# Norm boundaries of a one-core kernel: the last two weight pieces tile by tile, tile-step engine orders, rows turned by a diagonal

## The reference

```python
for i in range(2):
    h = _rmsnorm(x, norm_gains[i, 0])
    h = rwkv7_time_mix(h) if i == 0 else sgu_mixer(h)
    x = x + _rmsnorm(h, norm_gains[i, 1])
    h = _rmsnorm(x, norm_gains[i, 2])
    h = (silu(h @ w_gate) * (h @ w_up)) @ w_down
    x = x + _rmsnorm(h, norm_gains[i, 3])
h = rms_norm(x, norm1_g) * (1 + sc1) + sh1
x = x + g1 * (attention(h) @ w_out)
h2 = rms_norm(x, norm2_g) * (1 + sc2) + sh2
x = x + g2 * peer_ffn(h2)            # 128 experts for each token
```

## Time and profile before

| | us |
|---|---|
| median of 3 runs | 3378.89 (3374.46 to 3381.36) |
| the profiled execution's own time | 3387.03 |
| its span | 3385.0 |
| PE busy in it | 3175.8 (94%) |
| DVE, ACT, POOL busy | 2050.3, 1287.1, 776.2 |
| DMA, mean | 159 GB/s |

### The profile page before, as it was taken

How to read it: one execution, slowest core, us unless ns; L and a number is a source line. 1 busy time by engine, 2 the same in 40 slices (tenths; PEclk the granted TensorE clock), 3 DMA queues, 4 the chain that set the end, 5 groups by cost and what they waited for, 6 DMA issues and landing times.

```text
span 3385.0 us, 42343 instructions
## 1 busy us (share of the span) xinstructions
PE 3175.8 (94%) x16625; PEld 2715.6 (80%) x16625; DVE 2050.3 (61%) x3698; ACT 1287.1 (38%) x2171; POOL 776.2 (23%) x495
## 2 busy tenths in 40 slices
PE   8878999988999898999989999999999997999999
PEld 6456988977888776888878577999999896887777
DVE  5485656554332444333247655888888685887777
ACT  4454434434232323322234433335445452333332
POOL 0000011000000020000000300377676752354453
PEclk9888999999999987999999599999999998999999
DMA  3022112133333321333322002378878888999997
GB/s 132 24 77 75 57 57 69 57 106 93 95 99 97 97 80 57 94 99 96 97 81 83 3 26 94 101 255 290 304 267 304 281 295 304 360 340 350 329 354 272
DMA packets 229208, 537.63 MB, mean 159 GB/s; under 512 B 22337, under 2 KB 88129, under 8 KB 227474
## 3 DMA queue, kind: packets, MB, share of 16 engines
q1 hardware_dynamic: 191570, 398.57, 35.6%
q0 software_dynamic: 37440, 136.36, 11.0%
HBM read 482.40 MB, written 52.46 MB: 158 GB/s over the span
## 4 chain that ended last, share of the span: by engine, by line
PE 66%; DVE 13%; DMA 11%; ACT 4%; POOL 3%; issue 2%; SPq 1%; DVEq 0%; ACTq 0%
PE bank L339 22%; PE bank L342 14%; PE bank L2174 8%; DMA gl<-acts 6%; DMA eu<-in_peer_u 4%; PE bank L2602 3%; POOL etl L2162 3%; DVE vsl L2646 2%; PE bank L952 2%; DVE y_row L2219 2%; PE bank L962 2%; PE bank L1749 2%; PE bank L2331 1%; PE bank L916 1%; PE bank L904 1%
## 5 line engine op out<-in xcount | busy, mean ns | idle before, releaser
L294 DVE TENSOR_TENSOR wl<-raw,wh 128x1024 fp32r<-128x1024 f32 (+3 forms) x239 | 294.0, 1233 | 674.0 <-ACT wh L279 673.8
L279 ACT CAST wh<-raw 128x1024 fp32r<-128x1024 f32 (+3 forms) x239 | 247.1, 1036 | 676.5 <-PE bank L339 363.8
L2162 POOL TENSOR_TENSOR etl<-eu,eth 128x1024 fp32r<-128x1024 f32 x128 | 317.1, 2478 | 444.9 <-ACT eth L2158 443.9
L2174 PE MATMUL bank<-peerhh,eth 128*128 128x384 f32 x1024 | 350.2, 342 | 29.7 <-POOL etl L2162 25.4
L2174 PE MATMUL bank<-peerhl,eth 128*128 128x384 f32 x1024 | 344.4, 336 | 0.0
L2174 PE MATMUL bank<-peerhh,etl 128*128 128x384 f32 x1024 | 344.3, 336 | 0.0
L2602 PE MATMUL bank<-vsh,coefh 128*128 128x512 f32 x768 | 302.4, 394 | 20.0 <-DVE coefl L2657 19.9
L2602 PE MATMUL bank<-vsh,coefl 128*128 128x512 f32 x768 | 301.2, 392 | 0.0
L2602 PE MATMUL bank<-vsl,coefh 128*128 128x512 f32 x768 | 301.1, 392 | 0.0
L2199 POOL DMA_INDIRECT taken<-in_peer_v,gb x128 | 231.6, 1809 | 287.5 <-DVE y_row L2219 259.2
L2158 ACT CAST eth<-eu 128x1024 fp32r<-128x1024 f32 x128 | 135.5, 1059 | 235.2 <-DMA eu<-in_peer_u 234.6
(11 more groups left out here) (565 smaller groups left out, 7451.3 us busy)
## 6 DMA issues: line engine op xcount, KB each, us to landing
eu<-in_peer_u SPq DMA_DIRECT2D x128, 512.0 KB, 4.5
vb<-in_peer_v SPq DMA_DIRECT2D x128, 512.0 KB, 5.7
raw<-in_ada_w SPq DMA_DIRECT2D x48, 512.0 KB, 3.9
acts<-eg SPq DMA_DIRECT2D x128, 192.0 KB, 3.6
coefs<-stage SPq DMA_DIRECT2D x12, 2048.0 KB, 9.6
gd<-coefs SPq DMA_DIRECT2D x16, 1536.0 KB, 14.7
gl<-acts SPq DMA_DIRECT2D x128, 192.0 KB, 6.6
raw<-in_ffn_w_gate SPq DMA_DIRECT2D x44, 512.0 KB, 3.6
```

The source lines that it names most:

```text
L279: act.copy(parts_of(c)[0], raw_of(c)).then_inc(*up("w rounded", c))
L294: dve.tensor_tensor(lo, raw_of(c), hi.bitcast(F32), ALU.subtract).then_inc(*up("w split", c))
L2162: pool.tensor_tensor(Et[j % 3][1], Eu[j % 2], Et[j % 3][0].bitcast(F32), ALU.subtract).then_inc(*up("u split", j))
L2174: t = pe.matmul(b, tb[un][:, k * 128:(k + 1) * 128], peer_h[hn][:, k, 1:4, :], start=k == 0 and i == 0, stop=k == 7 and i == 2)
```

## The change

1. `pe_gemm(apart=True)`, for `wo`, both `down` and `sgu out`: in the last group the last two pieces are one step. PE does, for each output tile, both pieces before it goes to the next tile, so that the tiles finish 12 matmuls apart; the last one finishes where it did.
2. `evac_gemm(later=True)` for the same products: the last group's takes leave it, and the work ahead of its last piece is left out there (it is done behind the rows). `act_rows` and `dve_rows` now go by tile: take, post sum and mean, root, reciprocal, addition for tile s, then squares or mean of tile s-1, then root or scale of tile s-2.
3. Rows are no longer scaled. DVE multiplies `ident` by the 128 reciprocals into a 128 x 128 diagonal (`diag`, in `gb1`), and PE turns and norms in one: a float32 product of X's block with the diagonal. PE does row tiles 0 to 2 for ft 0 to 3, then for ft 4 to 7, then row tile 3 for all eight.
4. Waits that named the scaled rows name the filled banks: the load of `gb1` at b = 2 on SP (L1385), and ACT's use of `aa` at b = 0 (L759).

```diff
+            steps = [[c] for c in group]
+            if apart and gi == len(groups) - 1:
+                steps[-2:] = [group[-2:]]
+            for step in steps:
+                for (_, q, j, m), (b, before) in zip(tiles, got):
+                    for c in step:
...
+            rows_take = later and gi == len(groups) - 1
             for c in group:
+                if not (rows_take and c == group[-1]):
+                    ahead(c + 1 + AHEAD)
...
+            if not rows_take:
+                for tile in tiles_of(kind, groups)[gi]:
+                    take(*tile)
...
+    def act_rows(act, on_act, b, rows, x_ready, take=None):
...
+        for s in range(NT + 2):
+            if take and s < NT:
+                take(1, s, 512, 512)
+                c0 = small[:, 320 + 2 * s:321 + 2 * s]
+                on_act.wait_ge(*at("post mean", b, s))
+                act.sqrt(c0, c0).then_inc(*up("act root", "post", b, s))
+            if 1 <= s <= NT:
+                squares(s - 1)
+            if s >= 2:
+                root(s - 2)
...
+        def scale(tt):
+            c = small[:, tt:tt + 1]
+            on_dve.wait_ge(*at("act root", "row", b, tt))
+            dve.reciprocal(c, c).then_inc(*up("dve step", "row rstd", b, tt))
+            on_dve.wait_ge(*at("dve step", "row rstd", b, tt))
+            on_dve.wait_ge(*at("constants in"))
+            dve.tensor_scalar(diag[:, tt, :], ident, c, None, ALU.mult).then_inc(*up("row scale", b, tt))
...
+        for s in range(NT + 2):
+            if take and s < NT:
+                add(s)
+            if 1 <= s <= NT:
+                mean(s - 1)
+            if s >= 2:
+                scale(s - 2)
...
+    def pe_turn_rows(pe, on_pe, b, emptied):
+
+        got = [banks.take(("rows", b, ft), *emptied(ft)) for ft in range(KD)]
+        for tts, fts in ((range(3), range(4)), (range(3), range(4, 8)), ((3,), range(8))):
+            for tt in tts:
+                on_pe.wait_ge(*at("row scale", b, tt))
+                for ft in fts:
+                    p, before = got[ft]
+                    if tt == 0:
+                        for what in before:
+                            on_pe.wait_ge(*at(*what))
+                    t = pe.matmul(p[:, tt * 128:(tt + 1) * 128], X[:, tt, ft * 128:(ft + 1) * 128], diag[:, tt, :],
+                                  start=True, stop=True)
+                    if tt == NT - 1:
+                        t.then_inc(*up("bank full", "rows", b, ft))
...
-        on_sp.wait_ge(*at("v normed dve", NG - 1))
+        on_sp.wait_ge(*at("bank full", "rows", 2, KD - 1))
```

More of the change, by code:

```diff
@@ L309, in tiles_of, with pe_gemm @@
         return got
-    def pe_gemm(pe, on_pe, kind, plan, operand, ready, emptied, beside=None):
+    def pe_gemm(pe, on_pe, kind, plan, operand, ready, emptied, beside=None, apart=False):
         groups = st.plans[plan]
@@ L350, in pe_gemm, with evac_gemm @@
+    def evac_gemm(kind, plan, ahead, take, beside=None, later=False):
+        groups = st.plans[plan]
+        at_piece = 0
+        for gi, (_, _, group) in enumerate(groups):
+            rows_take = later and gi == len(groups) - 1
+            for c in group:
+                if not (rows_take and c == group[-1]):
+                    ahead(c + 1 + AHEAD)
                 if beside:
@@ L443, in pe_turn_rows @@
-    def pe_turn_rows(pe, on_pe, b, rows, emptied):
-        for ft in range(KD):
-            p, before = banks.take(("rows", b, ft), *emptied(ft))
-            for what in before:
-                on_pe.wait_ge(*at(*what))
-            for tt in range(NT):
-                on_pe.wait_ge(*at(*normed(b, tt)))
-                t = pe.transpose(p[:, tt * 128:(tt + 1) * 128], rows[:, tt, ft * 128:(ft + 1) * 128], ident)
-            t.then_inc(*up("bank full", "rows", b, ft))
+    diag = gb1[:, 0:512].rearrange("p (t n) -> p t n", t=4)
@@ new lines, in program, with squares, root @@
+    row_junk = f("row junk", 4, D)
+    def act_rows(act, on_act, b, rows, x_ready, take=None):
+        def squares(tt):
+            for what in x_ready(tt):
+                on_act.wait_ge(*at(*what))
+            if take and tt:
+                on_act.wait_ge(*at("row squares", b, tt - 1))
+            act.activation(row_junk if take else rows[:, tt, :], X[:, tt, :], ACT.Square,
+                           accum_out=small[:, tt:tt + 1]).then_inc(*up("row squares", b, tt))
+        def root(tt):
+            c = small[:, tt:tt + 1]
+            on_act.wait_ge(*at("row mean", b, tt))
+            act.sqrt(c, c).then_inc(*up("act root", "row", b, tt))
+        for s in range(NT + 2):
[8 more added lines that the diff above has]
+                root(s - 2)
@@ L758, in fin @@
                 else:
-                    on_act.wait_ge(*at("rows normed dve", 0, 3))
+                    on_act.wait_ge(*at("bank full", "rows", 0, KD - 1))
                     act.activation(aa[:, j, :], b, ACT.Sigmoid, bias=vec("a0", j)).then_inc(*up("aa", j))
@@ L1273, in act_gated @@
             act.copy(yF[0][:, ft, :], gy[ft % 2]).then_inc(*up("x rounded", "gated", ft))
-        evac_gemm("T", "wo", cast, act_post(act, on_act, 1, "wo", junk0, [("bank full", "gated", KD - 1)]))
+        evac_gemm("T", "wo", cast, act_post(act, on_act, 1, "wo", junk0, [("bank full", "gated", KD - 1)]),
+                  later=True)
     def dve_gated(dve, on_dve, rest):
@@ L1448, in act_sgu @@
         evac_gemm("T", "sgu out", cast,
-                  act_post(act, on_act, 3, "sgu out", junk0, [("tile full", "sgu u", 1, 3)]))
+                  act_post(act, on_act, 3, "sgu out", junk0, [("tile full", "sgu u", 1, 3)]), later=True)
     def dve_sgu(dve, on_dve, rest):
-        dve_rows(dve, on_dve, 2, sgu_rows, ffn_rows)
+        dve_rows(dve, on_dve, 2, ffn_rows, dve_takes[2])
         rest(st.plans["sgu v"][0][2][0] + AHEAD)
@@ L1520, in dve_sgu @@
         split(7)
-        evac_gemm("T", "sgu out", rest, dve_post(dve, on_dve, 3, "sgu out", sgu_rows, []))
+        evac_gemm("T", "sgu out", rest, dve_post(dve, on_dve, 3, "sgu out", sgu_rows, []), later=True)
     def pool_sgu(pool, on_pool):
```

195 lines of the change are left out of this document (76 added, 119 removed).

## The result

| | before | after |
|---|---|---|
| median | 3377.05 us (3374.12 to 3381.36, 5 runs) | 3353.19 us (3348.53 to 3359.94, 5 runs) |
| profiled execution | 3387.03 us, span 3385.0, clock 0.956 | 3353.19 us, span 3351.4, clock 0.968 |

The ratio is 0.9924 (95% interval 0.991 to 0.9939), a gain of 25.7 us with 20.6 to 30.4 as its interval; the two medians lie 23.9 apart. The forecast was 17.8. The sign held, the size did not: the measured median lies at the very edge of the range (3353 to 3373).

What follows compares the result with a forecast made beforehand. PE holds 66% of the chain and waits at boundaries for ACT and DVE, 70.4 us over four. Gains 21.0 at b = 1 to 4, -4.2 at b = 0, +1.1 at b = 5 sum to 17.9: 3361.1 us, range 3353 to 3373.

Steps and rivals of the forecast that it cites:

- PE's chain behind each boundary is unchanged, so I take the gain as kept to the end: Stages behind the boundaries: nothing added or taken back, so the summed gain of 17.9 us reaches the end.
- I take the clock as falling: Turning at b = 1 to 4: clock falls to half, back at T0+8 (T0: last matmul's end); next product starts T0+12.0.
- b5: Last boundary: scaling goes, DVE's passes and not the banks set later k-tiles; start 1.1 us earlier (3 earlier to 5 later).
- Tiles 12 matmuls apart, at no cost: Product ahead of each boundary: tiles end at T0-8.2, -5.4, -2.7 and T0, T0 unmoved; at most 1 us cost.
- The chain of one tile: ACT and DVE steps behind the last tile: addition ends T0+3.15, squares T0+4.3, diagonal T0+5.1; DVE takes 2.7 us a tile.
- rival (2): DVE is the pace, small steps at 0.24 us: four boundaries each 2 us later, gain 10, 3369 us; chance 0.13.
- The turning: PE at each boundary: 32 products, 64 instructions, twice a transpose's price; 7.1 us at 2.4 GHz, 13.8 at 1.2 GHz.
- Rival (4): Turning: a product costs four transposes, 0.436 us at full clock, 0.85 at half; 3396 us; chance 0.03.
- rival (1): Boundaries: clock stays up or is back sooner; starts at T0+10.4 for b = 1 to 3; about 3355 us; chance 0.20.
- b0: First boundary: 24 products precede the first full bank, first `h` at about 18 us; loss 4.2 us (bounds 1 and 8).
- (3): Turning: the products don't bring the clock back; with it down throughout, 3401 us; chance 0.06.
- (5): Takes are late: tiles end 12 apart but a piece's cast holds ACT or DVE; 3372 us or so; chance 0.06.

Runs made afterwards that it cites:

- by transposes: Changed kernel, but rows scaled into a buffer again and transposed with ident, new orders and tiles 12 apart kept: 3369.77 us, ratio 0.9949 to the kernel before.
- not apart: Changed kernel with the last two pieces one after the other again, so tiles finish 6 matmuls apart: 3387.75 us, ratio 1.0017 to the kernel before.
- diagonal alone: Kernel before, old orders, with scaled rows and transposes replaced by products with a diagonal of the row's scale: 3396.13 us, ratio 1.0036 to the kernel before.
- five memsets: Changed kernel with five idle 1024-column memsets on VectorE, one behind the other, ahead of the first boundary's parts: 3367.98 us.

## Why the prediction was right and wrong

Three steps failed. The largest is a term that the forecast put at nothing: "PE's chain behind each boundary is unchanged, so I take the gain as kept to the end"; the attention stage changed by 9.1 us with the clock granted in it. The second is "I take the clock as falling" at all four boundaries; it stayed up at three of them, worth 4.0. The third is b5, forecast as a gain of 1.1 and measured as a loss of 3.1. The last two cancelled by luck. The first is what moved the total, and the edit does nothing in that stage.

**The boundaries b1 to b4** came out at 11.8, 10.6, 10.7 and 11.4 from T0 where 12.0, 12.0, 12.0 and 13.4 were forecast.
- *Tiles 12 matmuls apart, at no cost*: right. The squares of the four tiles start 2.72 apart, the product's end doesn't move (358.9 for an FFN in both), and without this part the change gives nothing.
- *The chain of one tile*: right to a few tenths. Addition's end T0+3.1 (forecast 3.15), squares' start T0+3.1 and end T0+4.2 (4.3), last diagonal T0+5.3 (5.1), diagonals of 0.29 (0.27), first products at T0+0.9 (0.8) and T0+3.6 (3.5). DVE kept up; rival (2) fell.
- *The turning*: right. 64 instructions, 0.112 each at full clock (0.224 a product), on the path behind tile 2. Rival (4), four transposes to a product, fell. The Trainium skill ("TensorE: Matmul & The Clock Gate", Terms) gives the mode for float32 transposes as four times faster; the trace doesn't agree, if a float32 product is what that is measured against: 0.109 against 0.224 is twice.
- *The clock*: here a step failed. "I take the clock as falling and as back at T0+8": at b1 it fell, and was back at T0+7.2, near enough; at b2, b3 and b4 it never fell. The forecast took this fall for all four; the traces gave it at one and rival (1), with its T0+10.4, at the other three. That is 4.0 of the 4.9 us by which the sum of the four was off; b4 also lay 0.7 nearer to b2 and b3 than forecast (11.4 - 10.7 against 13.4 - 12.0), so its k-tiles were taken too slow by that. What was missed is that PE's idle time had gone from ten us in one piece to 0.9 and 1.6 in two. The row on which the fall was based, 762 to 772, was one of a PE that does nothing. The other kernels bear this out: where PE was idle for 3.6 us or more in one piece, the clock fell at all four boundaries (by transposes, not apart, diagonal alone, before); in every trace in which it was idle for 0.9 and 1.6 at all four, it fell at one of them.

**b0**: loss 3.9 where 4.2 was forecast, first `h` at 18.09 where "about 18" was. Right, by its own step: 24 products ahead of the first full bank.

**b5**: gain 1.1 forecast, loss 3.1 measured. The sign was wrong, and the step is one that the forecast had got right for b0 a paragraph earlier. "DVE's passes and not the banks set when the later k-tiles come": true, they are 1.52 apart before and after, but the first of them waits for a full bank, and that is now the one behind 24 other products. In the kernel before DVE began here:

```profile
2056.49 1.66 DVE L477 TENSOR_SCALAR shifted<-bank,small 128x512 f32<-128x512 f32 x2 [0.85 <-PE bank L450]
```

That is 8.4 us behind the last matmul's start (2056.49 - 2048.06); in the changed kernel it was 10.9 (2029.26 - 2018.37), and its whole row of passes with it. In all thirteen traces with the new order of turning at b5 the first q product starts 6.3 us behind that first pass, wherever the pass falls (9.9 to 12.4), with transposes too (11.05 and 17.34): what sets b5 is when the first bank is full, and with all row tiles turned before it that is late at either price. PE then waits 0.8 to 0.95 us for each of them, and the granted clock falls a second time (0.71 over 2034.4 to 2036.4, then 0.50), which is the 1.5 in the q products: they took 91.1 to 91.3 in every kernel with such a fall at their start and 89.6 to 90.1 in those without.

**What lay outside the sum**: 9.1 us of the attention stage, the largest miss. "I take the gain as kept to the end" looked at PE's chain, which is indeed unchanged, and not at its clock, for which the earlier trace rows had a row at half speed in this very stage (1917.42). The forecast used it as a price and didn't ask what would happen to the stretch.

So, stage by stage against the profiled execution of before: forecast 21.0 at the four boundaries, measured 25.9; b0 -4.2 and -3.9; b5 +1.1 and -3.1; not forecast: attention +9.1, small shifts of the stages between -1.3; sum 17.9 and, before rounding, 26.6, with which the measured 25.7 agrees. Without attention it is 17.6, so near to 17.9 by luck: errors of +4.9 and -4.2 cancelled. With the attention stage's clock held up in both kernels it was 15.0 in the traces. Rival (1) was the likeliest reading of the boundaries after all, at 0.20; rivals (3), (4) and (5) found nothing for them.

**What stays open.** Why the clock, once down in the attention stage, comes back after 51 us in one kernel and 75 in another, with the same instructions in the same order. The values 75.1 and 51.2 repeated in the second traces of the two kernels, and none goes with anything that I varied on purpose. Filling the wait removes the question and doesn't answer it. The same holds for b1, b3 and the gated and sgu stages, where 1.1 to 1.6 us come and go with the clock in some kernels and not in others.

## What to carry to other kernels

When a chain of small steps stands between two products, let the last product end tile by tile, so far apart that the slowest engine of the chain just keeps up; with the tiles no longer apart 22 of the 26 us were gone here, and with scaled rows instead of the diagonal 3. The same order of turning in a place where the rows don't come tile by tile out of a product (b0, b5) is a loss, because it makes the first result wait for the last tile: ask at each place when the first bank is full, not when the last one is. And in a profile read the granted clock of every stretch, not of the changed ones alone: waits of 3.9, 0.8 and 1.2 us in one place cost 18 to 27 us behind them, as much as the whole change was meant to gain, and 37 products of no use gave them back.

## What the runs showed of the hardware

- At the same busy share the granted clock was 0.50 in one kernel and 1.00 in another. In the attention stage of the changed kernel PE was busy for 45.0 of 47 us at 0.50 throughout; with the waits ahead of it filled, it was busy for 45.6 of 47 at 1.00 throughout, in the same stage. The Trainium skill ("TensorE: Matmul & The Clock Gate", Part 1) describes the gate as one that follows how busy TensorE has been of late; the first of these two rows does not agree with that, if busy is what the profile calls so.
- The times at 0.50 in that stage were 51.2, 58.0, 61.4, 68.3 and 75.1 us. The first stands in six traces, the third in three and the last in four, each the same to 0.1, and the first two of these on more than one chip; 58.0 and 68.3 stand in one trace each.
- Equal idle pieces gave unequal clocks: 0.89 and 1.56 us idle at b1 and at b2, a fall at the one and none at the other, in both traces of the changed kernel. With five memsets ahead, everything 6.8 us later, b1 took 11.0 without a fall and b3 12.7 with one. The Trainium skill ("TensorE: Matmul & The Clock Gate", Part 1) says that the gate keeps a rhythm of its own that doesn't start with the kernel. That a mere shift moved the fall agrees with it; that both traces of the changed kernel fell at the same boundary is not explained by it.
- Transposes alone brought the clock back again, as in the kernel before. At b1 of the kernel that turns by transposes PE has nothing else between the fall and the next product, which starts at 780.27:

```profile
777.00:779.20 2.20, 2.20 (x12) 2.20 (x11) 0.00 (x0) 0.55 (x1) 0.00 (x0) 0.50 0.52 119
779.40:780.20 0.80, 0.37 (x4) 0.14 (x2) 0.80 (x2) 0.80 (x2) 0.00 (x0) 1.00 0.58 223
```

The Trainium skill ("TensorE: Matmul & The Clock Gate", Part 4) says that the full clock doesn't engage for transposes; these rows do not agree.
